# Attention's entry in another order: prompt keys and first maxima ahead of the last page sums, two key units inside TensorE's waits, small copies on ScalarE

## The chip, the cores and the metric

The kernel runs on one core of a Trainium2 chip. The metric is the device time of one execution in microseconds; of several executions the median counts. Names of engines: TensorE (PE), VectorE (DVE), ScalarE (ACT), GpSimd (POOL) and SyncE (SP), which issues most of the DMA transfers. ScalarE issues some of its own.

## What is computed

One inference step of a two-layer decoder: 256 prompt tokens and 8 sample tokens (264 columns together, T). Layer 0 mixes with Mamba-2, layer 1 with native sparse attention; each is followed by a mixture of experts. The change lies in layer 1's attention. Cut to what matters:

```python
q, kv4, kvw, gates = nsa_project(h, w_in)          # one projection for all tokens
past_cmp = kv_pool[page_table, :, 0:2]              # sample tokens: 8 pages of 128 rows each
kc, vc = nsa_compress(cmp_rows, pos_w)              # sum of 64 rows, each times softmax(pos_w)
s_c = q . kc - slope * dist;  p_c = masked_softmax(s_c);  o_c = p_c @ vc
imp = p_c.sum(axis=3)                               # picks the selected blocks
s_s = q . ks - slope * dist;  p_s = masked_softmax(s_s);  o_s = p_s @ vs   # selected blocks
s_w = q . kw - slope * dist;  p_w = masked_softmax(s_w);  o_w = p_w @ vw   # window of 512
o = gates[0] * o_c + gates[1] * o_s + gates[2] * o_w
return o @ w_out
```

## The kernel before

Everything is laid out with features on the 128 partitions. The attention stage is written by hand as one instruction list for each engine; the engines meet only through semaphores, so each list's own order decides what is held up by what. Nothing is rearranged by a scheduler.

*Page sums.* For each of the 8 sample tokens (`b`, batch 0 to 7) eight pages of compressed keys and values are loaded into one of three buffers. VectorE multiplies two of four slices by the position weights, GpSimd the other two (`cmp_multiply`, line 136), and VectorE sums all four over blocks of 64 (`cmp_sum`, line 140). `compress(b)` does this for one batch and raises `c_used`. The buffers are then reused for the page keys: unit 0's load waits for `c_used` 6, unit 1's for 7, unit 2's for 8.

*Projections.* TensorE makes 21 tiles (`NT`, line 1771, eight products of 264 columns each); ScalarE copies each out of its bank into `qT`, `kvT` or `gT_` (lines 2010 to 2014) and raises `tile_taken`. From tile NT-4 on it issues, between the tiles, the 16 page loads of key unit 1 (`load_kv_group`, line 1677).

*Prompt keys.* VectorE copies the sample queries into `qbd` (line 2107, `q_ok`), weights and sums the prompt's keys (`ctmp`, `kc`, lines 2112 and 2115) and spreads them into `kcx` and `vx` (lines 2120 and 2121, `kc_ok`).

*Scores of the prompt.* There are 32 units (16 pairs) of one head and one of two branches. `score(pair)` (lines 1780 and 1783) makes the scores of two units; `soft(u)` on VectorE (lines 2133 to 2135) adds the distance bias and takes the two negative maxima; `exps(u)` on ScalarE takes the exponents; `scale(u)` (line 2141) and GpSimd (line 1755) weight them; `turn(u)` (line 1792) transposes them; `values(pair)` (lines 1803 to 1810) multiplies by the values. `score(pair)` waits for the maxima of the pair before.

*Keys and values of the pages.* Twelve load units go through five buffers: units 0 to 3 are page keys of 2 MB (16 transfers, but for the window units 4, 5, 8 and 11 of 4 transfers each), units 6 to 11 values and window values. `dec_keys(j)` (line 1825, eight products) uses key unit j, `dec_window` (line 1852) units 4 and 5, `dec_values` (line 1896) units 6 to 11. Each raises `kv_used`, for which the load that reuses its buffer waits on SP. `read_odd` reads 16 page numbers into SP's registers (line 127).

*The loop.* For each pair TensorE does `score(pair + 2)`, at pairs 0, 1, 2 and 4 `dec_keys(0)`, (1), (2) and (3), then `turn`, `values` of the pair before, `turn`. Ahead of the loop stand `score(0)`, the transposes of the prompt's values (line 1912), of the gates (1916) and of the new values (1919), the 16 compressed scores (line 1926, behind `kc_ok`), eight transposes of `vx` (line 1931) and `score(1)`. VectorE takes the gates and new values out of their banks (`gtok`, `vnew`, lines 2197 and 2199), and later the transposed compressed values (`vci`, lines 2216 and 2217). In a timeline each product counts as two records.

## Time and profile before

| | us |
|---|---|
| median of 3 executions | 1043.51 |
| lowest and highest | 1043.34, 1045.84 |
| the profiled execution's own time | 1046.67 |
| its span in the profile | 1044.6 |
| TensorE busy | 992.2 (95%) |
| VectorE, ScalarE, GpSimd busy | 492.4, 333.9, 186.0 |
| data moved by DMA | 343.20 MB, mean 329 GB/s |

All times of the trace are microseconds from the start of the span; the attention stage lies between about 545 and 745. The busy share of TensorE is high nearly everywhere, but a busy engine is not one at full speed: the granted clock is shown apart, as a share of 2.4 GHz. An idle time counts only where nothing else would have held the next step back, so each wait has to be read with what ended it.

### The profile page before, as it was taken

The page shows a single profiled execution, that of the slowest core. Times are in us where ns is not written, and L with a number is a line of the kernel's source. Part 1 is how long each engine was busy: PE and PEld are TensorE (multiplying, and loading weights), DVE is VectorE, ACT ScalarE, POOL GpSimd, SP SyncE. Part 2 cuts the span into 40 slices and gives each one's busy share as a digit, 9 for nine tenths or more (in the row PEclk, how much of TensorE's full clock was granted, in tenths as well). Part 3 has the DMA queues.
Part 4 walks back from the last instruction along what each step waited for, and adds up shares of the span by engine and source line. Part 5 has one row for each costly group of instructions (what it writes and reads, how often), then busy time and mean ns, then how long its engine had stood idle before and what let it go on. Part 6 is the DMA issues. An engine that isn't in the chain of part 4 may idle for free. (4 is left out here: it accounts for less than half of the span.)

```text
span 1044.6 us, 14969 instructions
## 1 busy us (share of the span) xinstructions
PE 992.2 (95%) x5181; PEld 618.9 (59%) x5181; DVE 492.4 (47%) x1422; ACT 333.9 (32%) x875; POOL 186.0 (18%) x201
## 2 busy tenths in 40 slices
PE   8999999899999999998999987979999999999897
PEld 6888776788744444443678864545874444444365
DVE  2889898771521111110479996671152111111056
ACT  3212888720451111110341013672045111112034
POOL 0000016321130000000345541441103000000033
PEclk9999999999999999999999995999999999999999
DMA  9963788669779999999827995959976999999974
GB/s 324 314 220 115 230 265 274 245 213 405 305 286 424 428 426 426 425 427 427 330 99 276 392 341 166 314 174 366 428 332 253 426 426 427 424 428 426 426 301 207
DMA packets 90144, 343.20 MB, mean 329 GB/s; under 512 B 15890, under 2 KB 53906, under 8 KB 73170
## 3 DMA queue, kind: packets, MB, share of 16 engines
q1 hardware_dynamic: 80074, 319.48, 78.8%
q10 hardware_dynamic: 7688, 18.39, 5.0%
q0 software_dynamic: 2304, 4.33, 1.2%
q8 instruction: 44, 0.72, 0.3%
q14 instruction: 34, 0.28, 0.1%
HBM read 331.56 MB, written 23.04 MB: 339 GB/s over the span
## 5 line engine op out<-in xcount | busy, mean ns | idle before, releaser
L1528 DVE TENSOR_TENSOR gates_and_hidden<-bank,gates_and_hidden 128x512 f32<-128x512 f32 x16 | 11.1, 692 | 310.6 <-PE bank L1179 310.6
L1179 PE MATMUL bank<-expert_ring,x_packed 128*64 128x512 f32 x320 | 118.3, 606 | 0.0
L1160 PE MATMUL bank<-expert_ring,x_packed 128*64 128x512 f32 x416 | 112.9, 593 | 1.1 <-DMA expert_ring<-in_moe_w_gate 0.8
L559 PE MATMUL ss<-xT,expert_ring 128*128 128x264 f32 x384 | 89.3, 392 | 4.7 <-DMA expert_ring<-in_ssd_w_in 4.7
L559 PEld LDWEIGHTS ss<-xT,expert_ring 128*128 128x128 f32 x384 | 72.9, 192 | 18.4 <-DMA xT<-in_xT 4.1
L1160 PEld LDWEIGHTS bank<-expert_ring,x_packed 128*64 128x64 f32 x416 | 36.8, 137 | 73.6 <-issue 73.6
L1389 POOL DMA_INDIRECT x_rows_packed<-x_rows,slot_token_int x16 | 16.3, 1020 | 334.8 <-DVE gates_and_hidden L1493 288.5
L1771 PE MATMUL bank<-xT,expert_ring 128*128 128x264 f32 (+1 forms) x324 | 72.7, 387 | 0.3 <-PEq L1006 0.3
L1523 DVE TENSOR_TENSOR acc<-acc,bank 128x264 f32<-128x264 f32 x128 | 54.9, 429 | 37.0 <-PE bank L1216 35.2
L1201 PE MATMUL bank<-expert_ring,gates_and_hidden 128*64 128x512 f32 x256 | 70.9, 596 | 1.4 <-ACT gates_and_hidden L1350 1.4
L1771 PEld LDWEIGHTS bank<-xT,expert_ring 128*128 128x128 f32 (+1 forms) x324 | 60.3, 187 | 12.7 <-issue 1.0
L1216 PE MATMUL bank<-gates_and_hidden,y_slots 128*128 128x264 f32 x256 | 60.3, 388 | 2.1 <-issue 2.1
L571 PE MATMUL ss<-xT,expert_ring 128*128 128x264 f32 x256 | 61.2, 393 | 0.7 <-ACT expert_ring_b L437 0.7
L1272 PE MATMUL bank<-slot_onehot,expert_ring 128*128 128x266 f32 x256 | 58.5, 387 | 0.0
L571 PEld LDWEIGHTS ss<-xT,expert_ring 128*128 128x128 f32 x256 | 47.4, 190 | 13.3 <-issue 4.3
L1216 PEld LDWEIGHTS bank<-gates_and_hidden,y_slots 128*128 128x128 f32 x256 | 45.6, 190 | 14.2 <-issue 5.4
L1272 PEld LDWEIGHTS bank<-slot_onehot,expert_ring 128*128 128x128 f32 x256 | 48.5, 190 | 9.0
L1332 ACT ACTIVATE y_slots<-bank 128x512 f32<-128x512 f32 x32 | 19.1, 597 | 106.6 <-PE bank L1201 95.6
L667 PE MATMUL ss<-conv_out,expert_ring 128*128 128x264 f32 x224 | 51.6, 387 | 0.9 <-issue 0.9
L1350 ACT ACTIVATE gates_and_hidden<-bank 128x512 f32<-128x512 f32 x16 | 9.6, 597 | 131.8 <-PE bank L1186 131.8
L1179 PE MATMUL bank<-expert_ring_d,x_packed 128*64 128x512 f32 x96 | 46.2, 630 | 5.2 <-DMA expert_ring<-in_moe_w_up 5.2
L1201 PEld LDWEIGHTS bank<-expert_ring,gates_and_hidden 128*64 128x64 f32 x256 | 21.7, 137 | 44.6 <-issue 42.7
(419 smaller groups left out, 1829.3 us busy)
## 6 DMA issues: line engine op xcount, KB each, us to landing
expert_ring<-in_moe_w_gate SPq DMA_DIRECT2D x26, 2048.0 KB, 20.0
expert_ring<-in_moe_w_up SPq DMA_DIRECT2D x18, 2048.0 KB, 21.1
expert_ring<-in_moe_w_down SPq DMA_DIRECT2D x16, 2048.0 KB, 19.9
expert_ring<-in_ssd_w_in SPq DMA_DIRECT2D x9, 2048.0 KB, 9.1
expert_ring_b<-in_moe_w_gate SPq DMA_DIRECT2D x6, 2048.0 KB, 17.6
expert_ring_c<-in_moe_w_up SPq DMA_DIRECT2D x6, 2048.0 KB, 22.4
expert_ring_d<-in_moe_w_up SPq DMA_DIRECT2D x6, 2048.0 KB, 20.9
expert_ring_c<-in_moe_w_down SPq DMA_DIRECT2D x6, 2048.0 KB, 22.6
```

Source lines behind the costliest of these rows:

```text
L559: last = mm(pt[m % 4][:, 0:T], wc[:, k, ((m - 1) % 4) * P:((m - 1) % 4 + 1) * P], xT[:, k, :], start=k == 0, stop=k == KD - 1)
L571: last = mm(z_bank[:, 0:T], wc[:, k, (j % 4) * P:(j % 4 + 1) * P], xT[:, k, :], start=k == 0, stop=k == KD - 1)
L667: last = mm(o_bank[m][:, 0:T], w_row(k)[:, m * P:(m + 1) * P], cv[:, k, :], start=k == 0, stop=k == JX - 1)
L1160: last = mm(hb[0][s * CAP:(s + 1) * CAP, :], xg[:, k, s * CAP:(s + 1) * CAP], unit(6 * i + s)[:, k * FF:(k + 1) * FF], start=k == 0, stop= ...
L1179: last = mm(hb[1][s * CAP:(s + 1) * CAP, :], xg[:, k, s * CAP:(s + 1) * CAP], unit(6 * i + 2 + s)[:, k * FF:(k + 1) * FF], start=k == 0, s ...
L1201: last = mm(ob[2 + a][s * CAP:(s + 1) * CAP, :], ht[:, k, s * CAP:(s + 1) * CAP], unit(6 * i + 4 + s)[:, o:o + 512], start=k == 0, stop=k ...
L1216: mm(bank[:, 0:T], ys[:, d * P:(d + 1) * P], sgt[:, i, :], start=True, stop=True).then_inc(sc_done, 1)
L1272: last = mm(gate_bank[m % 6][:, 0:T + 2], wc[:, k, (m % 4) * P:(m % 4 + 1) * P], scaled[:, k, :], start=k == 0, stop=k == KD - 1)
L1332: A_(ys[:, a * 512:(a + 1) * 512], ob[2 + a][:], ACT.Copy).then_inc(ys_ok, 1)
L1389: nc.gpsimd.indirect_dma_start(xrow[:, i % 2, :], None, x_rows[L][:, :], bass.IndirectOffsetOnAxis(idxi[:, i:i + 1], 0), bounds_check=T - ...
L1523: V.tensor_tensor(acc[:, d, :], acc[:, d, :], bank[:, 0:T], ALU.add).then_inc(acc_ok, 1)
L1771: last = mm(pb[m % 8][0:M, 0:T], wc[:, k, (m % 4) * P:(m % 4) * P + M], xT[:, k, :], start=k == 0, stop=k == KD - 1, skip_group_check=m == 0)
```

## The change

SP: after unit 4, `read_odd(1)`, then unit 5 behind `kv_used` 1, then units 2 and 3; the later units as before. ScalarE: the loads of unit 1 are issued in one block behind all tiles. VectorE: `compress` is split into `weigh` (the wait and the multiplies) and `add_up` (the sums); batch 7 is weighed behind the query copies and added up behind `soft(1)`. The copies `gtok`, `vnew` and `vci` go from VectorE to ScalarE. TensorE: `dec_keys(0)` behind `score(0)`; the gates' transposes use bank 5 instead of bank 6; four products of the identity with `xT` are added, whose results nobody reads; `score(1)` ahead of the `vx` transposes, `dec_keys(1)` behind them; `dec_keys(2)` and (3) at pairs 1 and 2. Two waits move: that for `gtok_ok` from `dec_keys(0)` to the `vx` transposes, that for `pct_ok` 2 from `dec_keys(1)` to `dec_keys(2)`.

```diff
     load_kv(sp, 4, page)
+    read_odd(1)
+    sp.wait_ge(kv_used, 1)
+    load_kv(sp, 5, page)
     sp.wait_ge(c_used, 8)
     load_kv(sp, 2, page)
-    read_odd(1)
     sp.wait_ge(tile_done, d0 + 20)
     load_kv(sp, 3, page)
-    for j in range(5, 12):
+    for j in range(6, 12):
         if j in (9, 10):
...
             pe.wait_ge(q_ok, 1)
-            pe.wait_ge(gtok_ok, 1)
-        if j == 1:
+        if j == 2:
             pe.wait_ge(pct_ok, 2)
...
     score(0)
+    dec_keys(0)
     vt = (V_SEL, V_SEL + 1, V_WIN, V_WIN + 1)
...
     for q in range(QT):
-        last = tr(dp[0][:, q * 48:(q + 1) * 48], gT_[:, q * P:(q + 1) * P], ident[0:48, 0:48])
+        last = tr(pt[5][:, q * 48:(q + 1) * 48], gT_[:, q * P:(q + 1) * P], ident[0:48, 0:48])
     last.then_inc(pre_tr, 1)
...
     last.then_inc(pre_tr, 1)
+
+    for _ in range(4):
+        mm(pt[4][:, 0:T], ident[:], xT[:, 0, :], start=True, stop=True)
...
     last.then_inc(csc, 1)
+    score(1)
+    pe.wait_ge(gtok_ok, 1)
     for i in range(KD):
...
     last.then_inc(pre_tr, 1)
-    score(1)
+    dec_keys(1)
...
             score(pair + 2)
-        if pair <= 2:
-            dec_keys(pair)
-        if pair == 4:
-            dec_keys(3)
+        if 1 <= pair <= 2:
+            dec_keys(pair + 1)
         if pair == 6:
...
                 act.dma_start(wgates, I["nsa_w_gates"]).then_inc(ld_chunk[c % 2], 16)
-        if m >= NT - 4:
-            if m == NT - 4:
-                act.wait_ge(c_used, 7)
-            load_kv_group(act, 1, m - (NT - 4), page)
+    act.wait_ge(c_used, 7)
+    for g in range(4):
+        load_kv_group(act, 1, g, page)
...
         A_(vtok[:, q, :], pt[2 + q][:], ACT.Copy).then_inc(vtok_ok, 1)
+    act.wait_ge(pre_tr, 3)
+    A_(gtok[:], pt[5][:, 0:96].rearrange("p (q c) -> p q c", q=QT), ACT.Copy).then_inc(gtok_ok, 1)
+    act.wait_ge(pre_tr, 4)
+    A_(vnew[:], dp[1][0:DB, :], ACT.Copy).then_inc(vnew_ok, 1)
     exps(0)
     exps(1)
+    act.wait_ge(pre_tr, 5)
+    A_(vci[:, 0:4, :], pt[5][0:64, :].rearrange("p (i m) -> p i m", i=4), ACT.Copy).then_inc(pct_ok, 1)
+    A_(vci[:, 4:8, :], dp[1][0:64, :].rearrange("p (i m) -> p i m", i=4), ACT.Copy).then_inc(pct_ok, 1)
     exps(2)
...
-    def compress(b):
+    def weigh(b):
         dve.wait_ge(ld_cmp[cmp_slot(b)], 16 * NPG * (b // 3 + 1))
...
         dve_step(dve, cmp_multiply(V, b, 1))
+
+    def add_up(b):
         cmp_sum(V, kcd, b, 0)
...
     dve_step(dve, i1)
-    for b in range(1, DB):
-        compress(b)
+    for b in range(1, DB - 1):
+        weigh(b)
+        add_up(b)
     dve.wait_ge(q_zero, 1)
...
     i1.then_inc(q_ok, 1)
+    weigh(DB - 1)
     dve.wait_ge(tile_taken, t0 + KD + 4)
...
-    dve.wait_ge(pre_tr, 3)
-    V.tensor_copy(gtok[:], dp[0][:, 0:96].rearrange("p (q c) -> p q c", q=QT)).then_inc(gtok_ok, 1)
-    dve.wait_ge(pre_tr, 4)
-    V.tensor_copy(vnew[:], dp[1][0:DB, :]).then_inc(vnew_ok, 1)
     soft(0)
     soft(1)
+    add_up(DB - 1)
     f = lambda t: t[:].rearrange("p q h n -> p (q h) n")
...
     V.tensor_tensor(f(pc), f(pc), bc, ALU.subtract).then_inc(cexp_in, 1)
-    dve.wait_ge(pre_tr, 5)
-    V.tensor_copy(vci[:, 0:4, :], pt[5][0:64, :].rearrange("p (i m) -> p i m", i=4)).then_inc(pct_ok, 1)
-    V.tensor_copy(vci[:, 4:8, :], dp[1][0:64, :].rearrange("p (i m) -> p i m", i=4)).then_inc(pct_ok, 1)
     for u in range(NU):
...
```

TensorE, from the end of the projections to the compressed probabilities' transposes. `expert_ring` is the buffer of the page keys, `expert_ring_c` holds `kvT`, `cmp_prompt_pairs` is `kcx`. Before:

```order
L1780 MATMUL bank<-expert_ring_c,expert_ring_b 128x128 x2
L1783 MATMUL bank<-expert_ring_c,expert_ring_b 128x256 x2
L1912 MATMUL bank<-ident,expert_ring_c 128x128 x8
...
L1926 MATMUL bank<-cmp_prompt_pairs,expert_ring_b 128x2x4 x16
L1931 MATMUL bank<-ident,gates_and_hidden 64x128 x8
L1780 MATMUL bank<-expert_ring_c,expert_ring_b 128x128 x2
...
L1825 MATMUL bank<-expert_ring 32x512 x8
L1792 MATMUL bank<-ident,gates_and_hidden 128x128 x6
L1974 MATMUL bank<-ident,cmp_probs 64x128 x2
```

Now:

```order
L1782 MATMUL bank<-expert_ring_c,expert_ring_b 128x128 x2
L1785 MATMUL bank<-expert_ring_c,expert_ring_b 128x256 x2
L1826 MATMUL bank<-expert_ring 32x512 x8
L1914 MATMUL bank<-ident,expert_ring_c 128x128 x8
...
L1925 MATMUL bank<-xT,ident 128x264 x4
L1931 MATMUL bank<-cmp_prompt_pairs,expert_ring_b 128x2x4 x16
L1782 MATMUL bank<-expert_ring_c,expert_ring_b 128x128 x2
...
L1938 MATMUL bank<-ident,gates_and_hidden 64x128 x8
L1826 MATMUL bank<-expert_ring 32x512 x8
...
L1794 MATMUL bank<-ident,gates_and_hidden 128x128 x6
L1979 MATMUL bank<-ident,cmp_probs 64x128 x2
```

The first key unit stands behind `score(0)`, the second ahead of `score(2)`, and none between `score(2)` and the transposes; the added products stand ahead of the compressed scores.

VectorE, from the multiplies of batch 7 to `soft(2)`. `cmp_dec` takes the page sums, `cmp_prompt` is `kc`. Before:

```order
L136 TENSOR_TENSOR expert_ring<-expert_ring,pos_softmax 128x8x128 x2
L140 TENSOR_REDUCE cmp_dec<-expert_ring 128x16 x4
L2107 COPY expert_ring<-expert_ring_b 64x8x4 x4
L2112 TENSOR_TENSOR s_sel<-expert_ring_c,pos_softmax 128x256 x4
L2115 TENSOR_REDUCE cmp_prompt<-s_sel 128x16
...
L2197 COPY gates_tok<-bank 128x96
L2199 COPY v_new<-bank 8x512
L2133 SCALAR_TENSOR_TENSOR gates_and_hidden<-expert_ring_b,bank 128x384
```

Now:

```order
L2121 COPY expert_ring<-expert_ring_b 64x8x4 x4
L136 TENSOR_TENSOR expert_ring<-expert_ring,pos_softmax 128x8x128 x2
L2127 TENSOR_TENSOR s_sel<-expert_ring_c,pos_softmax 128x256 x4
L2130 TENSOR_REDUCE cmp_prompt<-s_sel 128x16
...
L2148 SCALAR_TENSOR_TENSOR gates_and_hidden<-expert_ring_b,bank 128x384
L2149 TENSOR_REDUCE neg_max<-gates_and_hidden 128x1
...
L140 TENSOR_REDUCE cmp_dec<-expert_ring 128x16 x4
L2148 SCALAR_TENSOR_TENSOR gates_and_hidden<-expert_ring_b,bank 128x384
```

The four sums of batch 7 have gone from ahead of the query copies to behind the maxima of units 0 and 1, and the copies of gates and new values are no longer on this engine.

## Rows read from the trace of the kernel before

**Rows 1.** Windows: busy us of each engine (instructions), TensorE's clock, DMA share.
```profile
core 0: us, PE busy (x) PEld busy (x) DVE busy (x) ACT busy (x) POOL busy (x), PEclk, DMA share, GB/s
...
622.00:648.00 26.00, 18.36 (x86) 12.74 (x86) 18.18 (x51) 8.07 (x26) 3.03 (x6) 0.50 0.60 187
648.00:650.00 2.00, 2.00 (x14) 1.32 (x12) 1.50 (x7) 0.59 (x2) 0.37 (x1) 0.69 0.82 245
```

**Rows 2.** Timeline of TensorE: start us, us, line, output and inputs, records, idle.
```profile
611.73 6.30 PE L1771 MATMUL bank<-xT,expert_ring 128*128 128x264 f32 x27
...
622.13 1.97 PE L1912 MATMUL bank<-ident,expert_ring_c 128*128 128x128 f32 x8 [3.24 <-ACT expert_ring_c L2012]
...
630.62 6.99 PE L1926 MATMUL bank<-cmp_prompt_pairs,expert_ring_b 128*128 128x8 f32 x32 [5.04 <-DVE gates_and_hidden L2121]
...
639.88 1.06 PE L1783 MATMUL bank<-expert_ring_c,expert_ring_b 64*128 64x256 f32 x4
...
644.92 3.64 PE L1825 MATMUL bank<-expert_ring 128*32 128x512 f32 x16
...
649.85 0.49 PE L1780 MATMUL bank<-expert_ring_c,expert_ring_b 64*128 64x128 f32 x4
...
650.71 1.92 PE L1825 MATMUL bank<-expert_ring 128*32 128x512 f32 x16
...
655.80 1.92 PE L1825 MATMUL bank<-expert_ring 128*32 128x512 f32 x16
...
663.24 0.49 PE L1780 MATMUL bank<-expert_ring_c,expert_ring_b 64*128 64x128 f32 x4
...
667.71 0.49 PE L1780 MATMUL bank<-expert_ring_c,expert_ring_b 64*128 64x128 f32 x4
```

**Rows 3.** Timeline of VectorE, 612 to 667.
```profile
612.49 4.60 DVE L140 TENSOR_REDUCE cmp_dec<-expert_ring 128x16 f32<-128x1024 f32 x4
617.01 4.49 DVE L136 TENSOR_TENSOR expert_ring<-expert_ring,pos_softmax 128x1024 f32<-128x1024 f32 x2
621.53 4.60 DVE L140 TENSOR_REDUCE cmp_dec<-expert_ring 128x16 f32<-128x1024 f32 x4
626.05 0.76 DVE L2107 COPY expert_ring<-expert_ring_b 64x32 f32<-64x32 f32 x4
...
631.47 0.55 DVE L2133 SCALAR_TENSOR_TENSOR gates_and_hidden<-expert_ring_b,bank 128x384 f32<-128x384 f32 x1
...
633.37 0.41 DVE L2135 TENSOR_REDUCE neg_max<-gates_and_hidden 128x1 f32<-128x256 f32 x1
...
642.87 0.41 DVE L2135 TENSOR_REDUCE neg_max<-gates_and_hidden 128x1 f32<-128x256 f32 x1
...
644.21 0.67 DVE L2216 COPY vc_blockdiag<-bank 64x512 f32<-64x512 f32 x1
...
649.05 0.41 DVE L2135 TENSOR_REDUCE neg_max<-gates_and_hidden 128x1 f32<-128x256 f32 x1
...
666.64 0.41 DVE L2135 TENSOR_REDUCE neg_max<-gates_and_hidden 128x1 f32<-128x256 f32 x1
```

**Rows 4.** Timeline of GpSimd, its multiplies of batches 6 and 7.
```profile
607.99 11.30 POOL L136 TENSOR_TENSOR expert_ring<-expert_ring,pos_softmax 128x1024 f32<-128x1024 f32 x4 [8.11 <-DMA expert_ring<-in_cmp_pages]
```

**Rows 5.** Page loads of line 1677 by queue, 617 to 655, landing, SP's timeline.
```profile
L1677 ACTq DMA_DIRECT2D expert_ring<-in_ksel_pages x16: 339/340/483, 617.3 to 625.5; - x16
...
L1677 SPq DMA_DIRECT2D expert_ring<-in_ksel_pages x16: 332/333/343, 626.3 to 634.0; - x16
...
L1677 SPq DMA_DIRECT2D expert_ring<-in_ksel_pages x16: 332/333/1027, 643.7 to 651.5; - x16
...
DMA to landing us min/median/max: 2.0/2.4/6.0
...
654.48 12.01 SPq L1677 DMA_DIRECT2D expert_ring<-in_vsel_pages  x22
```

**Rows 6.** Window of the next stage's routing, columns as in the first group.
```profile
780.00:800.00 20.00, 18.57 (x87) 9.50 (x87) 8.02 (x12) 10.18 (x22) 9.99 (x10) 0.91 0.41 147
```

## The prediction

> **What bounds the kernel now.** I read the windows first, then TensorE's timeline, then VectorE's, then the two DMA queues. In the attention stage TensorE is the engine that others wait for, except at the entry. The projections and score(0) end at 618.9. Then TensorE waits 3.24 us for a tile that ScalarE takes late, does 3.45 us of small transposes (622.13 to 625.58, where the 5.04 us of idleness begin), and waits again until the compressed prompt keys are there, at 630.62 [rows 2]. It is at 0.50 of its clock from 622 to 648, after 3.1 us of idleness, that is 1.2 GHz instead of 2.4, and comes back only near 648.6 [rows 1, 2]. So the 16 compressed-score products cost 6.99 us, and the first unit of page keys 3.64 us where the second costs 1.92 [rows 2].
>
> The cause is VectorE's order. Batch 7 of the page sums is weighted from 617.01 and summed from 621.53 to 626.13; only then come the query copies, the prompt keys (until 630.6, when TensorE's wait for them ends) and the first maxima, soft(0) from 631.47 and soft(1) to 633.78 [rows 2, 3]. ScalarE is late for another reason: its 16 page loads, 617.3 to 625.5, stand between its last tiles [rows 5].
>
> Behind the entry all shifts together. The expert weights of the next stage are fetched when page buffers and PE's reads release them, and at 780 to 800 the DMA engines are only 0.41 busy [rows 6], so an earlier attention stage is an earlier end, one for one. The sum below is made against the profiled execution (span 1044.6, time 1046.67) and then taken off the median, which is 3.16 us lower.
>
> **The change, part by part.**
>
> *VectorE.* The copies to the query buffer (0.76 us [rows 3]) come first, from 617.1. The two multiplies of batch 7 then wait for GpSimd's, as now: 4.49 us for two that start at 617.01, with GpSimd done at 619.29 [rows 3, 4]. I take 621.7 for their end (about 1.2 us each once GpSimd is done). What now runs from 626.84 to 630.56 behind the query copies takes 3.7 us again, so the prompt keys are ready near 625.4. soft(0) and soft(1) take 2.3 us (631.47 to 633.78 [rows 3]), giving 627.7. The sums of batch 7 cost 4.60 [rows 3] and end at **632.3**, which is where the last key buffer comes free: now 626.13. Four copies go to ScalarE; the two of the compressed values, 0.67 each and overlapped by 0.07 (644.21 [rows 3]), take 1.2 us off VectorE's way to soft(4).
>
> *TensorE.* dec_keys(0) goes into the first wait: 1.92 us at full clock [rows 2], done near 621. The transposes take about half of their 3.45 us at full clock, and the four added products of 264 columns about 1.9 us (27 records of such products, two to a product, take 6.30 us: 0.47 a product [rows 2]); both are hidden in the wait for the prompt keys, which would otherwise be idle. They fit if they end by 625.4; with dec_keys(0) ended at 621, the transposes take until 622.8 and the added products until 624.7. Were that cover gone they would cost up to 1.9 us, 3.7 at half clock. The compressed scores then take 3.5 us at full clock or 6.99 at half [rows 2], ending near 629 or 633; score(1), the eight transposes and dec_keys(1) follow by 632.7 or 637. dec_keys(1) needs the load that ScalarE issues in one block, about 618.4 to 626.7 plus 2.4 to land: it is there by 629.1 [rows 5]. ScalarE's own small copies then end near 628.5, and its first exponents near 632 (both from the durations of the copies above and of VectorE's maxima, an estimate); nobody is waiting for them yet.
>
> *soft(2) to score(3).* soft(2) starts at 632.3 and soft(3) ends at 634.6 (now 643.28). From there to the end of soft(5) takes 6.2 us now (643.28 to 649.46 [rows 3]); without ScalarE's copies, and with score(2) at half clock, it takes 5.0 to 5.8. So score(3) starts near 640 instead of 649.85 [rows 2]. That is **ten microseconds gained, but they do not last.**
>
> *SP's queue.* This is the stall that is late next. The key pages of unit 2 wait for batch 7's sums, 632.3. Sixteen issues take 7.7 us from first to last (626.3 to 634.0), the next block starts 0.4 to 0.6 later, takes 7.8 more (643.7 to 651.5), and a page lands 2.4 after its issue [rows 5]. The page numbers, read now between the two blocks (their gap, 634.0 to 643.7, less one issue, is 9 us), are read before both, in the shadow of the wait for VectorE. So unit 2 lands near 632.5 + 7.7 + 2.4 = 642.6, unit 3 near 640.8 + 7.8 + 2.4 = **651.0**. The window keys of unit 5, now put ahead, cost the queue 1.85 us, over before 632.3.
>
> *Where PE meets it.* dec_keys(2) is ready near 641 to 642 and starts at 642.6. It and the rest of its pair take 5.1 us at full clock (650.71 to 655.80 [rows 2]); with 3 to 5 us of that at half clock PE is ready for dec_keys(3) at 649 to 650 and starts at 651.0. The same place in the loop, now dec_keys(2) of the third pair, is at 655.80 [rows 2]: **4.8 us gained**. From here on the same work follows, except that pair 4 has lost its key unit, 1.92 us. That pair lasts 4.47 now (663.24 to 667.71 [rows 2]), but soft(13), on which its end hangs, is done at 667.05 [rows 3], only 0.7 us before. So the pair gives about **0.7**, not 1.9. Together 5.5 us. SP begins the value pages at 649.2 instead of 654.5 [rows 5], 5.3 earlier, so the queue keeps pace with PE through the value units and the output weights.
>
> Unknown costs: the landing of unit 3 is bounded by 650.6 (2.0 to land) and 655 (6.0 [rows 5], a full queue; I take 2.4, the median). The pair-4 gain lies between 0 and 1.9. The copies on ScalarE lie between no cost and 1 us, if its longer chain reached score(2).
>
> **A rule against the trace.** The query copies start while GpSimd multiplies. In the trace VectorE's two-input multiplies that start beside GpSimd's take 4.49 us for two, but four one-input sums take 4.60 both beside it (612.49) and alone (621.53) [rows 3, 4]. I price the copies as one-input work, undisturbed. The Trainium skill (SBUF — State Buffer, section Who interferes with whom) says that the pair VectorE shares with GpSimd is an exclusive lock, and that a copy can take it as a multiply does, while a reduction never does. By that rule the copies wait until 619.29, the multiplies end at 622.5, and unit 3 lands at 651.8, which is the first rival below.
>
> **The rivals.**
> 1. *The copies wait for GpSimd* and everything behind is 0.8 us later: gain 4.7, **1038.8**. For it: the multiplies do wait. Against: the sums do not. Chance 0.18.
> 2. *The half clock eats the gain.* Gaps at 633, 636 and 641 keep TensorE at half clock through dec_keys(3). The second pair then ends at 642.6 + 3.6 + 6.1 = 652.3, dec_keys(3) at 655.9 instead of dec_keys(2)'s 657.7: 1.8 + 0.7 = 2.5 gained, **1041.0**. For it: 3.1 us of idleness lowered the clock, and ten microseconds of unbroken small products (630.62 to 640.94) did not lift it; only dec_keys(0), from 644.92, did, after some 3.7 us [rows 1, 2]. Against: dec_keys(2) is the same work and would lift it at about 646.3. Chance 0.15.
> 3. *It does not do what it says:* the entry is shorter but the queue of page loads sets the value units too, or a later wait swallows it; **1043.5**. Against: the queue itself runs 5.3 us earlier. Chance 0.09.
> 4. *Slower.* The same half clock, but not lifted before pair 5: the loop's pairs of 3.8 to 5.1 us have no long idle time, yet small waits could keep it down. Every two microseconds at half clock cost one; from 11 us at half clock behind dec_keys(3) the gain is gone, from 17 it is slower by over 0.3%. With 20 us: 5.5 − 10, **1048.0**. The low stretch now is 26 us long, with TensorE busy 18.4 of them [rows 1], but has no page keys until its end. Chance 0.07.
> 5. *More is gained:* the multiplies are not held by GpSimd (1.3 us earlier) and pair 4 gives its full 1.9: 4.8 + 1.3 + 1.9 = 8.0, **1035.5**. Chance 0.08.
>
> **How the numbers follow.** My forecast has 0.43: 1043.51 − 5.5 = 1038.0 (1041.2 for a profiled execution like this one). A measurement of this kernel tells about 0.3%, 3.1 us, from no change. Faster by more: forecast, rivals 1 and 5, 0.69. Within it: rivals 2 and 3, 0.24. Slower: 0.07. The range takes in the forecast, rivals 1 and 2 and most of 5, that is 8 times in 10: 1034.9 to 1042.0, with a microsecond's margin above rival 2.
>
> **What would show it.** In the changed profile: the prompt keys ready near 625.4; compressed scores start by 626.5; the sums of batch 7 end near 632.3; score(3) near 640; dec_keys(2) and dec_keys(3) each start on a DMA landing, near 642.6 and 651.0; the pair without a key unit lasts about 3.8; clock at 0.50 somewhere between 630 and 648. The prediction is wrong if dec_keys(3) starts later than 653, if the clock stays at 0.50 beyond 653, or if the value units begin less than 4 us earlier than now.

## The result, and the profile after

| | before | after |
|---|---|---|
| median of 6 executions each, run in turn | 1046.29 us | 1041.16 us |
| lowest and highest | 1043.34, 1048.2 | 1040.36, 1043.22 |
| ratio, 95% interval | | 0.9948 [0.9923, 0.9973] |
| profiled execution: its time, its span | 1046.67, 1044.6 | 1040.76, 1038.8 |

The forecast was a gain of 5.5 us, and the medians lie 5.1 apart. The absolute time, 1041.16, is 3.2 us above the forecast of 1038.0, because the kernel before measured 1046.29 over these six executions and 1043.51 over the three that the forecast started from. And the gain does not lie where the forecast had put it. TensorE's timeline of the two profiled executions, cut at `score(0)`, at the output projection and at the first expert product, gives:

| stage | before | after | gained |
|---|---|---|---|
| up to `score(0)` | 617.96 | 617.31 | 0.65 |
| `score(0)` to the output projection (attention) | 113.66 | 111.05 | **2.61** |
| output projection to the first expert product (routing) | 57.17 | 55.10 | **2.07** |
| from there to the end | 255.81 | 255.34 | 0.47 |

In this pair of traces attention gave half of what was forecast, and most of the rest came from a stage that the diff does not touch. One pair is little to go by: further traces of the same kernels (below) give attention between 2.6 and 5.1 us. TensorE's timeline of the changed kernel (columns as in [rows 2]; the line numbers are the changed kernel's: 1826 is `dec_keys`, 1931 the compressed scores):

```profile
617.31 0.49 PE L1782 MATMUL bank<-expert_ring_c,expert_ring_b 64*128 64x128 f32 x4
...
620.05 1.92 PE L1826 MATMUL bank<-expert_ring 128*32 128x512 f32 x16 [1.82 <-DVE expert_ring L2121]
...
623.62 1.95 PE L1925 MATMUL bank<-xT,ident 128*128 128x264 f32 x8
626.20 4.76 PE L1931 MATMUL bank<-cmp_prompt_pairs,expert_ring_b 128*128 128x8 f32 x32 [0.63 <-DVE gates_and_hidden L2136]
...
634.31 2.49 PE L1826 MATMUL bank<-expert_ring 128*32 128x512 f32 x16
...
640.69 0.41 PE L1979 MATMUL bank<-ident,cmp_probs 128*64 128x128 f32 x2 [2.23 <-DVE cmp_probs L2239]
641.80 0.49 PE L1782 MATMUL bank<-expert_ring_c,expert_ring_b 64*128 64x128 f32 x4 [0.70 <-DVE neg_max L2150]
...
644.44 3.64 PE L1826 MATMUL bank<-expert_ring 128*32 128x512 f32 x16 [1.46 <-DMA expert_ring<-in_ksel_pages]
...
653.12 1.92 PE L1826 MATMUL bank<-expert_ring 128*32 128x512 f32 x16 [1.31 <-DMA expert_ring<-in_ksel_pages]
...
660.57 0.49 PE L1782 MATMUL bank<-expert_ring_c,expert_ring_b 64*128 64x128 f32 x4
...
664.43 0.49 PE L1782 MATMUL bank<-expert_ring_c,expert_ring_b 64*128 64x128 f32 x4 [1.05 <-DVE neg_max L2150]
```

Against [rows 2] the entry is nearly as it was drawn: the compressed scores start 4.4 us earlier and take 4.76 instead of 6.99, `score(3)` starts at 641.80 instead of 649.85. Then eight microseconds of lead shrink to 2.7 at the fourth key unit, which stands where the third of [rows 2], 655.80, stood. Between 641.8 and 653.1 TensorE is slowed twice, by two waits for page keys and by its clock (windows, columns as in [rows 1]):

```profile
628.00:634.00 6.00, 6.00 (x34) 5.01 (x33) 5.97 (x9) 2.80 (x9) 0.00 (x0) 0.56 0.88 346
634.00:642.00 8.00, 5.07 (x36) 2.02 (x36) 6.18 (x24) 4.60 (x17) 3.12 (x7) 0.91 0.76 217
642.00:648.00 6.00, 4.54 (x24) 1.00 (x22) 3.40 (x16) 2.12 (x9) 3.22 (x6) 0.53 0.78 233
```

The one low stretch of 26 us has become two of some 6 us. VectorE's timeline of the changed kernel:

```profile
617.08 2.91 DVE L2121 COPY expert_ring<-expert_ring_b 64x32 f32<-64x32 f32 x4
620.02 2.36 DVE L136 TENSOR_TENSOR expert_ring<-expert_ring,pos_softmax 128x1024 f32<-128x1024 f32 x2
```

and the two queues that the forecast rested on, GpSimd's last multiplies and SP's issues:

```profile
608.06 11.30 POOL L136 TENSOR_TENSOR expert_ring<-expert_ring,pos_softmax 128x1024 f32<-128x1024 f32 x4 [9.28 <-DMA expert_ring<-in_cmp_pages]
```

```profile
633.16 17.57 SPq L1677 DMA_DIRECT2D expert_ring<-in_ksel_pages  x32
650.83 11.31 SPq L1677 DMA_DIRECT2D expert_ring<-in_vsel_pages  x22
```

The copies, 0.76 us in [rows 3], now take 2.91 and end 0.6 us after GpSimd's multiplies do (619.36): the first of the four takes 2.32 us, the other three under 0.2 each. SP's value pages begin 3.65 us earlier than in [rows 5].

### The profile page after: what moved, and what is told of

Read it like the earlier page. It is cut to its first block and busy times, and to the rows that moved or that the text cites. A ratio compares the mean times of both kernels' runs of the same rounds, so it can differ in the third digit from the quotient of the medians.

```text
span 1038.8 us, 14986 instructions
## 1 busy us (share of the span) xinstructions
PE 987.6 (95%) x5189; PEld 616.5 (59%) x5189; DVE 493.2 (47%) x1418; ACT 335.2 (32%) x879; POOL 184.5 (18%) x201
## 5 line engine op out<-in xcount | busy, mean ns | idle before, releaser
L1160 PEld LDWEIGHTS bank<-expert_ring,x_packed 128*64 128x64 f32 x416 | 36.7, 137 | 72.7 <-issue 72.7
```

The source lines that it names most:

```text
L1160: last = mm(hb[0][s * CAP:(s + 1) * CAP, :], xg[:, k, s * CAP:(s + 1) * CAP], unit(6 * i + s)[:, k * FF:(k + 1) * FF], start=k == 0, stop= ...
```

## The experiments

Each ratio is to the kernel before, measured on the same chip as the variant. Since `score(0)` itself starts anywhere from 615.5 to 619.8 over all traces, the stages are compared, not the spans. Attention, routing and rest are the stages of the table above; the times in the stage columns come from one trace each. All of them, in us:

| kernel | median | ratio to before | fourth key unit (before: third) after `score(0)` | attention | routing | last row write issued to gather | rest |
|---|---|---|---|---|---|---|---|
| before | 1046.29 | | 37.84 | 113.66 | 57.17 | 6.32 | 255.8 |
| before, again (e1) | 1046.02 | 0.9995 | 38.43 | 114.31 | 61.36 | 9.67 | 256.6 |
| after | 1041.16 | 0.9948 | 35.81 | 111.05 | 55.10 | 5.29 | 255.3 |
| after, again (e2) | 1039.11 | 0.9935 | 35.53 | 109.19 | 55.84 | 4.28 | 255.4 |
| query copies early (e3) | 1040.27 | 0.9951 | 34.36 | 111.07 | 55.86 | 4.28 | 255.8 |
| no added products (e4) | 1043.44 | 0.9978 | 35.44 | 109.10 | 56.71 | 4.74 | 255.4 |
| before, unit 8 held (e5) | 1048.35 | 1.0036 | 38.29 | 114.19 | 58.40 | 4.28 | 257.1 |
| after, unit 8 held (e6) | 1043.30 | 0.9987 | 35.73 | 109.39 | 60.70 | 4.28 | 256.5 |
| e3 + split + unit 8 held (e7) | 1044.51 | 0.9992 | 42.56 | 119.47 | 58.82 | 4.28 | 256.4 |
| no added products, again (e8) | 1041.79 | 0.9975 | 36.12 | 111.44 | 56.83 | 4.28 | 255.5 |
| split unit 3 (e9) | 1039.32 | 0.9932 | 36.24 | 109.90 | 55.78 | 4.28 | 255.4 |
| sums before maxima (e10) | 1039.31 | 0.9934 | 36.03 | 109.69 | 56.28 | 4.68 | 255.4 |
| before, unit 8 behind gather (e11) | 1042.91 | 0.9972 | 36.93 | 112.76 | 54.88 | 4.28 | 255.4 |
| after, unit 8 behind gather (e12) | 1040.24 | 0.9950 | 36.71 | 114.89 | 54.04 | 4.28 | 255.8 |

**Both kernels again.**

> The kernel before, unchanged, for a second trace of it. Question: in the first pair of traces TensorE reached the output projection 3.26 us earlier (731.62 and 728.36), but the first expert product 5.33 us earlier (788.79 and 783.46); where do the 2.1 us of the routing between the two come from? Theory A (the routing's length varies from run to run: the row gather's DMA, 5.47 against 4.43 us, and the half clock after TensorE's wait for it): in this trace the distance from the output projection's start to the first expert product is not again 57.2 us, but anywhere from 55 to 57.5. Theory B (it belongs to the kernel before): 57.2 again within 0.3. Time equal to the kernel before within 1 us.

> The changed kernel, unchanged, for a second trace and for the ratio. Theory A: the distance from the output projection to the first expert product is between 55 and 57.5 us and not tied to 55.1; the attention stage itself (start of score(0) to start of the output projection, 111.05 us in the first trace against 113.66 before) repeats within 0.3 us, since it hangs on instruction counts. Ratio to before 0.9975 if only the 2.6 us of the attention stage are real, 0.995 if the routing's 2.1 us are part of the change's effect.

Measured: 0.9995 [0.9975, 1.0014] and 0.9935 [0.9909, 0.9961]. The gain is real, 5 to 7 us. The two traces of each kernel agree on the place of the fourth key unit (third in before) within 0.6 us. None of the narrow expectations held: routing of before was not 57.2 again, nor within 55 to 57.5, and attention of the changed kernel did not repeat within 0.3. It varies by 1.9 (111.05, 109.19), and 1.57 of that is one piece of clock: behind a wait of 1.39 us that both have near 701, the first value unit takes 2.70 us in one trace and 1.93 in the other, where the clock stays up. It stays up there in five traces of the changed kernel and its variants (e2, e4, e6, e9, e10) and in none of the four of before and its variants.

Routing has such a piece too, with the opposite sign. The products of `acc` with ones in it (line 1070, sixteen records) take 3.81 us at full clock and up to 5.51 where the clock falls (after, after again):

```profile
760.53 3.81 PE L1070 MATMUL bank<-acc,ones 128*128 128x264 f32 x16
```

```profile
758.15 5.50 PE L1070 MATMUL bank<-acc,ones 128*128 128x264 f32 x16
```

The clock falls there in e2, e3, e4, e6, e8, e9 and e10, and then the last row write is issued 45.7 us behind the start of the output projection instead of 44.0. It does not fall in the first trace of the changed kernel, nor in any trace of before and its variants. So routing of 55.8 in e2 is 54.1 plus 1.7 us of half clock, while the 55.10 of the first trace is another sum. What decides which execution loses which piece is open. Routing is longer in both traces of before, and by some 6 us in the second.

**The query copies away from GpSimd's multiplies.** On VectorE alone, in `after`:

```diff
     for b in range(1, DB - 1):
+        if b == DB - 2:
+            ...the query copies, q_ok
         weigh(b)
         add_up(b)
-    ...the query copies, q_ok
     weigh(DB - 1)
```

> The changed kernel with VectorE's four query copies ahead of batch 6's multiplies, into the 2.4 us in which VectorE waits for pages and GpSimd is idle. In the changed kernel these copies took 2.91 us instead of 0.76, ending 0.6 us after GpSimd's last multiply. Theory (they are held up by GpSimd, and the end of the batch-7 sums sets the landing of key units 2 and 3): the copies take 0.76 us; dec_keys(0) starts at 618.5 instead of 620.05; the batch-7 sums end 0.8 to 0.9 us earlier, and so do dec_keys(2), dec_keys(3) and the output projection, 0.9 us. Rival (the copies are slow by themselves behind the sums, or the keys land by another cause): copies still near 2.9 us, or the sums earlier and dec_keys(3) not.

Measured 1040.27, 0.9951 [0.9925, 0.9977], no better than the changed kernel. VectorE's timeline of it:

```profile
603.15 0.76 DVE L2120 COPY expert_ring<-expert_ring_b 64x32 f32<-64x32 f32 x4
...
614.46 4.50 DVE L136 TENSOR_TENSOR expert_ring<-expert_ring,pos_softmax 128x1024 f32<-128x1024 f32 x2
```

Ahead of GpSimd's multiplies, which begin at 605.45 here, the same four copies take 0.76; beside them, 2.91. In the kernel with three edits the moved copies fell beside the multiplies of batch 6 (GpSimd 605.35 to 614.63), and took 9.20, some 2.3 us for each, which is what one of GpSimd's multiplies takes there:

```profile
605.47 9.20 DVE L2125 COPY expert_ring<-expert_ring_b 64x32 f32<-64x32 f32 x4
```

That settles rival 1's mechanism: in these traces a copy of 64x32 that starts beside a multiply of GpSimd's ends only with it. The edit also shows what it is worth. The fourth key unit starts at 34.36, 1.2 to 1.5 us earlier than in the changed kernel, but waits 2.83 us for its pages, and after that wait it runs at half clock:

```profile
649.97 3.34 PE L1826 MATMUL bank<-expert_ring 128*32 128x512 f32 x16 [2.83 <-DMA expert_ring<-in_ksel_pages]
```

3.34 us instead of 1.92: the wait is paid for once more, and nothing is left of the gain. The expectation, 0.9 us less, failed.

**No added products.** The four products of the identity with `xT` are left out (their results are read by nobody).

> The changed kernel without the four added products of the identity with xT, whose results nobody reads. Theory (they only keep the clock up a little longer, and the stretch behind ends at the landing of unit 3, set by SP): TensorE's clock falls to 0.50 some 1 to 3 us earlier, the compressed scores take 7.0 us instead of 4.76, dec_keys(1) ends some 2 us later, yet dec_keys(3) starts at 653.1 as before within 0.3 us, and the time is the same. Rival (the clock decides): dec_keys(3) 1 to 2 us later and the time 1 to 2 us longer.

Measured 0.9978 [0.9958, 0.9997], and the second time:

> The changed kernel without its four added products, again, since its first time (1043.44) lay 2.3 to 4.3 us above the changed kernel's two medians while its attention stage in the profile was no longer (109.10 against 111.05 and 109.19 us). If the added products are worth nothing, as the profile says: median within 1.5 us of the changed kernel (1039 to 1042.5) and attention stage of 109 to 111. If they are worth what the first time says: 1043 to 1044 again, and somewhere a stage that is 2 us longer.

0.9975 [0.9954, 0.9997], 1041.79. Both medians lie above those of the changed kernel, by 0.6 to 4.3 us, but attention does not show it (109.10 and 111.44). Without the products TensorE is idle for 2.42 us ahead of the compressed scores instead of 0.63 (first of the two traces), and these then take 4.67 us instead of 4.76, not the 7.0 that was expected, so the products did not keep the clock up for them there. In the second trace they take 5.77, but the clock had fallen already at the first key unit (3.00 us). What remains is a routing of 56.7 and 56.8 against 55.1 and 55.8: up to 1.7 us of each of the two is the half clock at line 1070 that the changed kernel's second trace has too, and the last microsecond lies between the row write and the first expert product, where two traces each settle nothing. What the added products are worth stays open between nothing and 4 us.

**Where routing's two microseconds come from.** In the windows of the routing the DMA engines tell the kernels apart (before, before again, after; the last two columns are DMA share and GB/s):

```profile
760.00:776.00 16.00, 14.85 (x104) 11.90 (x103) 10.40 (x42) 10.26 (x20) 0.00 (x0) 1.00 1.00 423
776.00:780.00 4.00, 3.49 (x24) 3.00 (x24) 2.39 (x15) 1.06 (x3) 0.00 (x0) 1.00 0.45 182
```

```profile
776.00:780.00 4.00, 4.00 (x25) 3.56 (x23) 2.12 (x15) 0.78 (x2) 0.00 (x0) 1.00 0.99 418
```

```profile
776.00:780.00 4.00, 4.00 (x24) 3.47 (x22) 2.53 (x7) 0.78 (x2) 2.02 (x2) 1.00 0.14 25
```

From some 716 on the engines move the next experts' weights at some 423 GB/s without a gap. Read from windows of two microseconds, that stream ends near 777.8, 781.1 and 774.9 (estimates). Meanwhile ScalarE writes the token rows to DRAM (line 1309), and GpSimd gathers them (line 1389) once the last write has landed and VectorE has made the token index (line 1485). The last write is issued at 775.64, 773.99 and 772.38, and the gather starts 6.32, 9.67 and 5.29 us later; where the stream is over in time it is 4.28. That 4.28 is the index, not the write: there the gather starts 0.96 us behind the index copy. Behind the same copy it starts 2.6, 6.4 and 2.0 us late in these three traces, so the write costs 1.6, 5.4 and 1.0 us. The row write stands in the stream of weights. TensorE then waits for the gather, and in both traces of before its clock falls, to 1.69 and 1.97 us for products that take 1.09 in the changed kernel (before, before again, after):

```profile
785.41 1.69 PE L1141 MATMUL bank<-ident,x_rows_packed 128*128 128x128 f32 x8 [1.43 <-DMA x_rows_packed<-x_rows,slot_token_int]
```

```profile
787.67 1.97 PE L1141 MATMUL bank<-ident,x_rows_packed 128*128 128x128 f32 x8 [5.78 <-DMA x_rows_packed<-x_rows,slot_token_int]
```

```profile
781.11 1.09 PE L1141 MATMUL bank<-ident,x_rows_packed 128*128 128x128 f32 x8 [0.83 <-DMA x_rows_packed<-x_rows,slot_token_int]
```

The Trainium skill (DMA: Bandwidth & Descriptors, the paragraph on arbitration) says that each DMA engine takes turns between its queues packet by packet. By that rule a write to DRAM is slowed beside the stream, not held until its end. In the three traces the gather starts 2.6 to 4.2 us behind the stream's end, though the write was issued 2.2, 7.1 and 2.5 us ahead of that end, which looks more like a hold; no run tells the two apart. To test it, the last 2 MB of the stream (unit 8, first needed by the second pair of experts) were held back, in both kernels:

```diff
     load_unit(sp, L, 3 + 2 * L, unit(3 + 2 * L))
+    if L == 1:
+        sp.wait_ge(r_rows, 96)
     load_unit(sp, L, 8, unit(8))
```

> The kernel before with one load held back: in layer 1 the weights of a second-pair expert (load unit 8, 2 MB, needed only some 50 us later) are issued once the token rows are written to DRAM, instead of at 761.5. Theory F (the stream of expert weights sets the gather): in four traces the gather starts 2.5 to 3.2 us after the stream's end (before 778.7 and 781.96, before again 781.1 and 783.66), and where the stream had ended early it starts 4.3 us after the last row write is issued. With 2 MB less, 4.9 us at 427 GB/s, the stream ends near 774 and TensorE's own work decides: gather 4.3 to 5 us after its write, from o-proj to the first expert product 55.1 to 55.9 us instead of 57.2 to 61.4, kernel 2 to 4 us faster than before. Rival R (routing only varies by chance): the distance stays at 57 to 61 and the time within 1 us of before. Rival S: the held load comes too late for the second pair, a wait of 2 us or more there takes the gain back.

> The changed kernel with the same load held back. Theory F: the stream ended at 774.9 and 773.1 in its two traces, near the point where TensorE decides (0.83 and no wait at the gather), so only 0 to 1 us is left to gain; the distance from o-proj to the first expert product is 55.1 to 55.9 as without the edit, and the advantage of this kernel over the kernel before with the same edit is that of the attention stage alone, 2.6 to 4.5 us. Rival R: no difference to the changed kernel either, and the advantage over the kernel before with the same edit stays at 5 to 7 us.

Both became slower than without the edit: 1.0036 [1.0015, 1.0056] and 0.9987 [0.9968, 1.0005]. From the write to the gather it is 4.28 us in both, as forecast, and with no stream beside it the write is quick: the load that it releases is issued 1.8 us behind it (775.95 to 777.74 in before's variant). But the gather starts at 780.23, behind that release, so that the load ran beside it. TensorE waited 2.81 and 3.45 us for the gather, then worked at half clock:

```profile
782.88 1.97 PE L1143 MATMUL bank<-ident,x_rows_packed 128*128 128x128 f32 x8 [3.45 <-DMA x_rows_packed<-x_rows,slot_token_int]
```

The theory had the price of the write right and forgot the second small transfer. Another 1.2 us are lost behind the first expert product in each (257.1 and 256.5). And one number speaks against the theory: with the write freed in both kernels, the medians are still 5.0 us apart (1048.35 and 1043.30). The expectation had put 2.6 to 4.5 there if the stream explained the routing, and 5 to 7 if it did not. Since both variants also have the new wait at the gather, it is no clean test. In the next edit the wait is `sp.wait_ge(row[0], 16 * (4 * L + 1))`, the landing of the gather:

> The kernel before; unit 8 is held back as in the earlier experiment, but until the first gather has landed, so that it can't stand beside it. There, released with the last row write, it ran during the gather and TensorE waited 2.8 to 3.5 us for it. Theory F (any stream of weights beside the row write or the gather lengthens routing): with neither overlapped, the gather starts 4.3 us after its write and lands 3.4 us later, from o-proj to the first expert product 55.1 to 55.9 us instead of 57.2 and 61.4, and the kernel is 2 to 4 us faster than before. Rival B (the 2 MB are missed later, since the stream of weights is full from 790 on): the routing is as short, but what is behind it grows from 255.8 to 258 us or more, and the time is no lower.

> The changed kernel with unit 8 held back until the first gather has landed, the edit that took the kernel before to a routing of 54.88 us and a median 3.2 us lower. Theory F: in the changed kernel the stream of expert weights ends early enough in most executions (routing 55.1 to 55.9 us with the weights as they are), so the edit has only 0 to 1 us left to give: routing 54.9 to 55.3, time 1038 to 1040.5, below the kernel before by 6 to 8 us. The advantage over the kernel before with the same edit (1042.9) is then the attention stage's own, 2.6 to 4.5 us. Rival: the two gains add up in full (2 us or more below the changed kernel, under 1037.5), which would mean that the earlier end of the stream is not part of what the change gained.

In the kernel before the gather starts 4.28 us behind the write (775.27), and TensorE's wait for it is down to 0.61 us, without a fall of the clock behind it:

```profile
779.55 1.09 POOL L1391 DMA_INDIRECT x_rows_packed<-x_rows,slot_token_int  x1 [21.80 <-DVE slot_token_int L1487]
```

```profile
783.77 1.09 PE L1143 MATMUL bank<-ident,x_rows_packed 128*128 128x128 f32 x8 [0.61 <-DMA x_rows_packed<-x_rows,slot_token_int]
```

Routing takes 54.88 us, nothing is lost behind it (255.4), and the median is 3.2 us below before: 0.9972 [0.9948, 0.9995]. In the changed kernel the same edit gives nothing: 0.9950 [0.9927, 0.9973] against 0.9948 and 0.9935 without it, though its routing is as short, 54.04; it lies 5.1 us below before, where 6 to 8 were expected. Its own profiled execution has a long attention, 114.89, whose clock is at 0.50 from 704 to 710.

So the stream is worth 3.2 us to the kernel before (0.5 to 5.4 by the interval), and in the two traces of the changed kernel it ends early enough to cost the write 1 us or nothing. How much of the measured gain that is, the runs leave open. With the edit in both kernels 2.7 us are left between the medians (1042.91 and 1040.24, on two chips; 1.9 when each is taken from the kernel before on its own chip). With the earlier edit in both it was 5.0. The intervals of the ratios are some 2 us wide to either side and hold both readings. The traces put attention's part at 3.1 us on average, 113.7 over four traces of before and its variants against 110.6 over eight of the changed kernel and its variants (e3 and e7 left out).

**What sets the fourth key unit.** Half of unit 3's page loads ahead of SP's wait for batch 7's sums:

```diff
     load_kv(sp, 5, page)
+    sp.wait_ge(tile_done, d0 + 20)
+    load_kv_group(sp, 3, 0, page)
+    load_kv_group(sp, 3, 1, page)
     sp.wait_ge(c_used, 8)
     load_kv(sp, 2, page)
-    sp.wait_ge(tile_done, d0 + 20)
-    load_kv(sp, 3, page)
+    load_kv_group(sp, 3, 2, page)
+    load_kv_group(sp, 3, 3, page)
```

> The changed kernel; only SP's order differs: half of key unit 3's 16 page loads are issued ahead of the wait for batch 7's sums, the other half behind unit 2. Theory Q (SP's queue sets dec_keys(3)): the fourth key unit starts 16 to 17 us after the end of batch 7's sums instead of 20.1 to 20.4, or when TensorE is ready for it, about 1.3 us before the old landing: 34 to 34.6 us after score(0) instead of 35.5 to 36.1, with no DMA wait over 0.3 us ahead of it. Time 1 to 1.5 us below the changed kernel, if nothing else moves. Rival C (contention): the eight extra loads meet ScalarE's sixteen of unit 1, both queues slow down as in the trace of the kernel with three edits (ScalarE's block 10.4 us instead of 8.4), unit 1 lands later and dec_keys(1) waits 2 to 3 us for it: no gain or a loss of up to 3 us.

Measured 1039.32, 0.9932 [0.9906, 0.9959]. The DMA wait ahead of the fourth unit is gone, and the unit starts no earlier, 36.24 us after `score(0)`, where 34 to 34.6 were expected:

```profile
644.98 3.64 PE L1829 MATMUL bank<-expert_ring 128*32 128x512 f32 x16 [1.58 <-DMA expert_ring<-in_ksel_pages]
...
652.84 0.80 PE L1785 MATMUL bank<-expert_ring_c,expert_ring_b 64*128 64x128 f32 x4
653.43 0.81 PE L1788 MATMUL bank<-expert_ring_c,expert_ring_b 64*128 64x256 f32 x4
654.17 1.92 PE L1829 MATMUL bank<-expert_ring 128*32 128x512 f32 x16
```

```profile
648.00:654.00 6.00, 6.00 (x28) 3.21 (x24) 0.00 (x0) 1.74 (x6) 0.00 (x0) 0.51 0.87 263
```

The third unit and the rest of its pair take 9.2 us at 0.5 to 0.6 of the clock, against the 5.1 at full clock of [rows 2]. Behind the queue stands the clock, and the two end within a microsecond or two of each other: in the first trace of the changed kernel TensorE was ready 34.5 us after `score(0)` and waited 1.31 for the pages, in its second trace the unit starts at 35.53 with no wait listed. The kernel with three edits at once tells less:

> The changed kernel with three edits: query copies ahead of batch 6's multiplies, half of key unit 3's 16 page loads issued by SP ahead of its wait for batch 7's sums (the other half behind unit 2), and unit 8 held back. Theory Q (SP's queue of 32 issues behind the sums sets dec_keys(3)): the fourth key unit starts 20.2 us after the end of batch 7's sums in three traces (632.99 and 653.12; 632.08 and 652.32; 629.56 and 649.97). With 8 fewer issues in between at 0.52 us each it would be 16; TensorE is ready some 2.8 us before the old landing, so the fourth key unit starts 2 to 3 us earlier against score(0) than with early query copies alone: 31.3 to 32.4 us after it instead of 34.4, and starts without a wait for DMA or with one below 0.5. Time 1.5 to 3.5 us below the changed kernel. Rival: the landing of unit 3 or the half clock behind it keeps the fourth key unit at 34 us or later and the time within 1 us of the changed kernel.

1044.51, 0.9992 [0.9969, 1.0014], executions from 1038.6 to 1053.5; the fourth key unit came after 42.56 us, where 31.3 to 32.4 were expected. The profiled one is a bad one (the copies' 9.20 us above; ScalarE's 16 issues took 10.43 us beside SP's, so `dec_keys(1)` waited 2.87), and its third edit is the one that cost 2 to 4 us by itself. It does not speak for or against the split.

**One part undone.** `add_up(DB - 1)` ahead of `soft(0)` and `soft(1)` again, in `after`.

> The changed kernel with one part undone: batch 7 is added up ahead of soft(0) and soft(1) again (the query copies and prompt keys stay in front). Theory Q: the sums end 2.3 us earlier, SP's 32 issues start 2.3 us earlier, so the fourth key unit's pages land 2.3 us earlier, 33.3 to 33.8 us after score(0); TensorE meets soft(1) 4.6 us later, though: score(2) waits for it until about 633.5 against score(0) at 617.3, and from there to dec_keys(3) it needs some 13 to 15 us. So dec_keys(3) starts 34 to 36 us after score(0), and the time is within 1.5 us of the changed kernel: that order buys nothing. Rival E (the early maxima are what the change lives from): dec_keys(3) 2 us or more later than in the changed kernel, and the time 2 to 5 us above it.

Measured 1039.31, 0.9934 [0.9909, 0.9959]. `score(1)` waits 1.93 us for the maxima and starts 17.0 us after `score(0)` instead of 13.6, yet the fourth key unit comes after 36.03 us, now without a DMA wait. So the first maxima ahead of the last sums buy nothing here. None of the variants is measurably faster than the changed kernel; the best medians of variants (1039.31 and 1039.32) lie between its own two. No run undoes the moved key units alone, so that they are what earns attention's part is read from the timelines, not shown by an experiment.

## Why the prediction was right, and where not

That 5.5 us were forecast and 5.1 measured is in part luck: the forecast put all of it into attention, whose part is 2.6 us in the first pair of traces and 3.1 on average, and a stage it had no term for made up the rest. Of its three signs of being wrong two came true, both narrowly: dec_keys(3) started at 653.12, later than 653, and the value units began 3.26 us earlier (706.01 and 702.75), less than 4.

- *The query copies, 0.76 us undisturbed.* Wrong: 2.91, the first rival. The rule of the Trainium skill cited there (SBUF — State Buffer, Who interferes with whom) agrees with the trace; pricing a copy by sums beside GpSimd did not. The multiplies took 2.36 behind them and ended at 622.4, as that rival said (622.5). The rival's size for the whole, 0.8 us later, fits the sums (0.7), but the landing came 2.1 later.
- *Prompt keys 625.4, soft(1) 627.7, sums 632.3.* 626.1, 628.4 and 632.99: 0.7 late throughout, all of it from the copies.
- *Added products and transposes hidden, dec_keys(0) near 621.* Held: 621.9 for its end, 625.6 for the products', 0.63 us of idle time left.
- *score(3) near 640.* 641.80. Of the ten microseconds eight were gained there, and they did not last, as said.
- *Unit 2 lands at 642.6, unit 3 at 651.0.* The step that failed. Both units start on landings, at 644.44 and 653.12. The sums were 0.7 late, and the 32 issues took 17.57 us, where 16.1 were counted from undisturbed blocks. So the third pair's place is 2.7 us earlier instead of 4.8, and 2.0 measured from `score(0)`. This is the first trace; in the second the third unit starts behind half clock (a first wait of 1.98 us for the second unit's pages) and not on its landing. Over all traces it is 1.9 (four of before and its variants 36.9 to 38.4, mean 37.9; eight of the changed kernel and its variants, without e3 and e7, 35.4 to 36.7, mean 35.95).
- *TensorE ready for dec_keys(3) at 649 to 650.* It was ready at 651.81, for the third unit started 1.8 us late and ran wholly at half clock (3.64 us). With the queue relieved (e9) this gave 36.24 in one execution. So the second rival, half clock behind gaps near 633, 636 and 641, was half of the truth: the gaps came (2.23, 0.70 and 1.46 us, from 638.5 to 644.4), and its 1.8 us is close to the 2.0 that the entry gained.
- *The pair without its key unit: 0.7, lasting 3.8.* Held: 3.86 instead of 4.47, ended by soft's maximum.
- *SP begins the value pages 5.3 earlier.* 3.65. The size was off, as the sign on the value units said.
- *"An earlier attention stage is an earlier end, one for one."* Wrong, in the fortunate direction. It was read from a window, 780 to 800 [rows 6], behind the stretch that counts. At 720 to 778 the DMA engines were full, and the row write in that stretch set the gather. The forecast had no term and no rival for it: 2.07 us in this pair of traces, of which 1.03 lie between the write and the gather and 1.04 behind it. What the stream costs the kernel before is 3.2 us by e11.

## What to carry to other kernels

Before an earlier stage is counted as an earlier end, look also for small transfers on the path (a write, a gather) that stand in a long stream of prefetched weights; the piece of the stream that nobody needs soon can go behind them, and behind all of them. Where a queue and a half clock end at the same place, relieving one shows nothing, so price both chains up to their meeting and forecast the later one. A wait that is shortened pays only if what follows it keeps its clock. And a stage's gain is not read from one pair of traces: here the same kernel's attention moved by 1.9 us and its routing lost or kept 1.7.

## What was not expected of the hardware

- One idle wait of 1.4 us near 701 was followed by half clock in some traces and by full clock in others of the same kernel: 2.70 and 1.93 us for the same value unit, 1.57 us of the attention stage. At line 1070 the same products took 3.81 us in some traces and 5.16 to 5.51 in others.
- Four copies of 64x32 elements, 0.76 us together, took 2.91 where one of them met a multiply of GpSimd's and 9.20 where all four did, while four sums of 128x1024 took 4.60 with and without them.
- A 2 MB load beside one small gather made TensorE wait 2.8 to 3.5 us, against 0.61 or nothing without the load.
